# Modulation weights in eight column groups, and five projection units accumulated k by k at the start of a hybrid decoder block

## The reference

```
mod = c @ w_ada + b_ada                       # c: 1 x 1024, w_ada: 1024 x 3072
shift, scale, gate = split(mod, 3)
h = rmsnorm(x, pre_norm_gain) * (1 + scale) + shift        # 512 x 1024
proj = h @ w_in                                # split into aq ak av az iq ik iw bq bk bv bz bbeta ba ga gb
y_a = (dsa_attention(rope(aq), rope(ak), av, ...indexer of iq, ik, iw...) * silu(az)) @ w_a_out
y_b = (rmsnorm(gated_delta_rule(conv(bq), conv(bk), conv(bv), g, beta)) * silu(bz)) @ w_b_out
out = (sigmoid(ga) * y_a + sigmoid(gb) * y_b) @ w_o
return x + gate * rmsnorm(out, post_norm_gain)
```

## Time and profile before

| | us |
|---|---|
| median of 3 runs (827.45 to 828.1) | 827.98 |
| span of the profiled execution | 824.1 |
| PE busy | 797.4 |
| VectorE busy | 439.9 |
| GpSimd busy | 393.3 |
| ScalarE busy | 330.6 |

### The profile page before, as it was taken

One profiled execution on the slowest core, in us unless ns is written; L12 is line 12 of the kernel. 1 busy time (PEld: TensorE's weight loads), 2 busy tenths in 40 slices (PEclk: granted clock), 3 DMA queues, 4 the chain that ended last, 5 costly groups with the idle time before them and its releaser, 6 DMA issues.

```text
span 824.1 us, 11189 instructions
## 1 busy us (share of the span) xinstructions
PE 797.4 (97%) x4060; PEld 639.8 (78%) x4060; DVE 439.9 (53%) x957; ACT 330.6 (40%) x701; POOL 393.3 (48%) x338
## 2 busy tenths in 40 slices
PE   6899899999999999999999999999999999999997
PEld 2377775787887888888887777777778788878997
DVE  5677779848779855776754333343343332331113
ACT  0557455543544435445335334424443322122231
POOL 0415643465545644545554453554365355434451
PEclk9999999999999999999999999999999999999999
DMA  8936656543344333333212212222222255542602
GB/s 314 345 104 213 163 116 168 157 118 104 95 82 113 72 103 104 89 89 90 78 51 78 78 52 76 83 74 75 77 77 73 61 173 182 176 128 77 215 17 102
DMA packets 166800, 95.61 MB, mean 116 GB/s; under 512 B 35009, under 2 KB 158274, under 8 KB 165722
## 3 DMA queue, kind: packets, MB, share of 16 engines
q1 hardware_dynamic: 166746, 94.91, 40.2%
HBM read 85.11 MB, written 9.22 MB: 114 GB/s over the span
## 4 chain that ended last, share of the span: by engine, by line
PE 77%; DVE 11%; DMA 4%; ACT 4%; issue 2%; SPq 1%; POOL 1%; DVEq 0%; POOLq 0%; ACTq 0%
PE ps L699 19%; PE ps L701 18%; PE ps L700 18%; DMA w_ada_sb<-in_w_ada 2%; PE ps L979 2%; PE ps L1030 2%; PE ps L1029 2%; PE ps L1028 2%; PE ps L966 2%; ACT prob L1278 2%; DVE prob L1917 1%; PE ps L973 1%; PE ps L817 1%; DVE kraw L1734 1%; PE ps L863 1%
## 5 line engine op out<-in xcount | busy, mean ns | idle before, releaser
L1376 POOL TENSOR_TENSOR w_lo<-raw,w_hi 128x512 fp32r<-128x512 f32 (+1 forms) x216 | 294.7, 1388 | 305.0 <-ACT w_hi L1052 289.6
L699 PE MATMUL ps<-h_hi,w_hi 128*128 128x512 f32 (+1 forms) x680 | 286.2, 421 | 1.1 <-DVE h_lo L1597 1.0
L701 PE MATMUL ps<-h_hi,w_lo 128*128 128x512 f32 (+1 forms) x680 | 266.7, 392 | 0.0
L700 PE MATMUL ps<-h_lo,w_hi 128*128 128x512 f32 (+1 forms) x680 | 265.4, 390 | 0.0
L699 PEld LDWEIGHTS ps<-h_hi,w_hi 128*128 128x128 f32 (+1 forms) x680 | 127.8, 188 | 32.1 <-issue 8.3
L701 PEld LDWEIGHTS ps<-h_hi,w_lo 128*128 128x128 f32 (+1 forms) x680 | 127.3, 187 | 28.8
L700 PEld LDWEIGHTS ps<-h_lo,w_hi 128*128 128x128 f32 (+1 forms) x680 | 128.1, 188 | 23.0 <-issue 2.2
L1052 ACT ACTIVATE w_hi<-raw 128x1024 fp32r<-128x1024 f32 (+1 forms) x109 | 113.6, 1051 | 19.4 <-PE ps L1030 17.1
L1218 ACT ACTIVATE o_tok<-ps 128x128 f32<-128x128 f32 x32 | 8.9, 278 | 92.8 <-PE ps L931 92.7
L1029 PE MATMUL ps<-w_lo,y_hi 128*128 128x256 f32 x128 | 36.2, 283 | 0.0
L1030 PE MATMUL ps<-w_hi,y_lo 128*128 128x256 f32 x128 | 36.2, 283 | 0.0
(11 more groups left out here) (276 smaller groups left out, 1330.7 us busy)
## 6 DMA issues: line engine op xcount, KB each, us to landing
raw<-in_w_in SPq DMA_DIRECT2D x84, 512.0 KB, 3.7
w_ada_sb<-in_w_ada SPq DMA_DIRECT2D x8, 1024.0 KB, 11.4
inverse_tiles<-zero SPq DMA_DIRECT2D x12, 344.0 KB, 4.8
raw<-in_w_b_out SPq DMA_DIRECT2D x8, 512.0 KB, 3.8
raw<-in_w_a_out SPq DMA_DIRECT2D x8, 512.0 KB, 3.8
ada<-in_w_ada SPq DMA_DIRECT2D x8, 512.0 KB, 5.0
raw<-in_w_o SPq DMA_DIRECT2D x8, 512.0 KB, 3.8
x_sb<-in_x SPq DMA_DIRECT2D x4, 512.0 KB, 20.0
```

The lines of the kernel that those rows point to most:

```text
L699: pe.matmul(out_ap, w_hi[:, slot, k, 0:m], rhs_hi(k), start=(k == 0), stop=False)
L700: pe.matmul(out_ap, w_hi[:, slot, k, 0:m], rhs_lo(k), start=False, stop=False)
L701: mm = pe.matmul(out_ap, w_lo[:, slot, k, 0:m], rhs_hi(k), start=False, stop=(k == KT - 1))
L1376: ins = pool.tensor_tensor(w_lo[:, slot, ks, 0:n], raw[:, slot, ks, 0:n], w_hi[:, slot, ks, 0:n].bitcast(F32), ALU.subtract)
```

## The change

Inputs are now laid out on the host before the launch: the columns of `w_ada` for shift and scale in eight groups (`w_mod`, group k holds the 128 shift and 128 scale columns that eighth k of `h` needs, for all 1024 rows), the weights of the first five units by k (`w_first`), those of the others unit by unit (`w_units`), and all per-channel vectors in one tile (`first_cols`).

The opening becomes a loop over the eighths. For eighth k, 1 MB of `w_mod` and 0.33 MB of `w_first` arrive. The sum over the 1024 rows is made in two stages: ACT multiplies the first of eight row blocks by its part of `c`, DVE adds the seven others (`mod_sum`, seven instructions of 128 x 256), and two matmuls of one column by ones (`modulation`) add over the partitions and leave shift and scale as columns in PSUM. DVE adds the bias and gain (`mod_columns`, two instructions of 128 x 1). ACT then makes h and `h_hi`, POOL makes `h_lo`, ACT and POOL split the 128 x 640 weights of the five first units for this k, and PE does 15 matmuls (`first_units`): five with the rounded parts, then ten with the rests. `S` and `K0` to `K3` lie in five banks of their own. The matmuls of `w_ada` on PE and those without a reader are gone. The rotary tables are computed for the 24 distinct frequencies, widened by DVE, and transposed by 16 PE transposes, which ACT copies out.

From then on the rounds are as before, but round 0 starts after five units instead of two, so there are 12 rounds fewer. `R_KEY` lets K0 to K3 begin in rounds 1, 4, 7 and 10, units GA3 and GA4 come ahead of the first delta head, and DVE does `small` (the columns of S) ahead of the K taps of a round.

```diff
 RING = 4
-K_VEC = 5
+N_FIRST = 5
+GROUPS = 5
+FIRST_RAW = 3
...
-UNITS = ([("S", 0), ("K", 0)] + [("K", h) for h in range(1, 4)] + [("I", n) for n in range(4)]
...
+UNITS = ([("S", 0)] + [("K", h) for h in range(4)] + [("I", n) for n in range(4)]
+         + MIDDLE)
...
-R_KEY = [ends_at("K", h) for h in range(HEADS)]
-R_LOW = [10, 11, 12, 13, 30, 33, 46, 50]
-R_GRAM = [11, 12, 13, 16, R_DELTA[0] + 1, R_DELTA[0] + 6, R_DELTA[1] + 3, R_DELTA[1] + 7]
-R_INV = [24, R_DELTA[1] + 12]
+R_KEY = [1, 4, 7, 10] + [ends_at("K", h) for h in range(4, HEADS)]
+R_LOW = [8, 9, 10, 11, 22, 25, 38, 42]
+R_GRAM = [9, 10, 12, 16, R_DELTA[0] + 1, R_DELTA[0] + 6, R_DELTA[1] + 3, R_DELTA[1] + 7]
+R_INV = [20, R_DELTA[1] + 12]
...
+    def bank_of(q):
+
+        if PROJ_BANKS <= q < N_FIRST:
+            return q
+        return ((q - N_FIRST if q >= N_FIRST else q) + FIRST_BANK) % PROJ_BANKS
+
+    def before_in_bank(q):
+
+        return q - PROJ_BANKS if q >= N_FIRST + PROJ_BANKS else q - N_FIRST
...
+        sp.dma_start(pos_i[:], positions).then_inc(s_pos, 16)
...
+        def conditioning(k):
+            if k >= GROUPS:
+                sp.wait_ge(*pro_pe.at(f"mod{k - GROUPS}"))
+            for n in range(2):
+                half = slice(n * KT // 2, (n + 1) * KT // 2)
+                sp.dma_start(mod_rows[:, k % GROUPS, half, :], w_mod[k, :, half, :]).then_inc(s_mod[k % GROUPS][n], 16)
+
+        def first_weights(k):
+            if k >= FIRST_RAW:
+                sp.wait_ge(*pro_pool.at(f"wl{k - FIRST_RAW}"))
+            sp.dma_start(first_raw[:, k % FIRST_RAW], w_first[k]).then_inc(s_first[k % FIRST_RAW], 16)
+
+        for k in range(KT):
+            conditioning(k)
+            first_weights(k)
...
+        def first_units(k):
+
+            last = k == KT - 1
+            pe.wait_ge(*pro_act.at(f"wh{k}"))
+            pe.wait_ge(*pro_act.at(f"hi{k}"))
+            for q in range(N_FIRST):
+                pe.matmul(bank(bank_of(q)), first_hi[:, k, q, :], h_hi[:, k, :], start=(k == 0), stop=False)
+            if not last:
+                modulation(k + 1)
+            pe.wait_ge(*pro_pool.at(f"wl{k}"))
+            pe.wait_ge(*pro_pool.at(f"lo{k}"))
+            for q in range(N_FIRST):
+                pe.matmul(bank(bank_of(q)), first_lo[:, k, q, :], h_hi[:, k, :], start=False, stop=False)
+                mm = pe.matmul(bank(bank_of(q)), first_hi[:, k, q, :], h_lo[:, k, :], start=False, stop=last)
+                if last:
+                    mm.then_inc(unit_done, 1)
+                if q == 1 and k + 2 < KT:
+                    turn(k + 2)
...
+        def modulation(k):
+
+            if k == 0:
+                pe.wait_ge(*pro_pool.at("ones"))
+            else:
+                pe.wait_ge(*pro_dve.at(f"scale{k - 1}"))
+            pe.wait_ge(*pro_dve.at(f"row{KT - 1}_{k}"))
+            for n in range(2):
+                mm = pe.matmul(ps[:, 5, 2 * k + n:2 * k + n + 1], mod_rows[:, k % GROUPS, 0, n * P:(n + 1) * P], ones_p[:, 0:1],
+                               start=True, stop=True)
+            mm.then_inc(*pro_pe.inc(f"mod{k}"))
...
-        def condition(ks):
-            for k in ks:
-                pe.wait_ge(s_ada[k], 16)
-                for n in range(4):
-                    pe.matmul(bank(2 + n), cb[:, k, :], w_ada_sb[:, k, n * S:(n + 1) * S], start=(k == 0), stop=False)
-
-        pe.wait_ge(*pro_dve.at("cb"))
-        condition(range(2))
-        pe.wait_ge(s_rows2, 16 * 5)
-        pe.transpose(ps[:, 7, P:P + 3], prow2[:], ident[0:3, 0:3]).then_inc(*pro_pe.inc("rows2T"))
-        condition(range(2, K_VEC))
-        pe.wait_ge(*pro_pool.at("ones"))
-        pe.wait_ge(*pro_dve.at(f"acc{KT - 1}"))
-        for n in range(4):
-            mm = pe.matmul(bank(2 + n), ones_p[:], w_ada_sb[:, K_VEC, n * S:(n + 1) * S], start=False, stop=True)
-        mm.then_inc(*pro_pe.inc("mod"))
-        for _ in range(3):
-            pe.matmul(bank(0), cb[:, KT - 1, :], w_ada_sb[:, KT - 1, 0:S], start=True, stop=True)
...
+        def first_row(k):
+            act.wait_ge(s_mod[k % GROUPS][0], (k // GROUPS + 1) * 16)
+            act.activation(mod_rows[:, k % GROUPS, 0, :], mod_rows[:, k % GROUPS, 0, :], ACT.Copy,
+                           scale=pcol[:, 0, R_C:R_C + 1]).then_inc(*pro_act.inc(f"row{k}"))
+
+        act.wait_ge(s_rows, 16)
+        first_row(0)
+        act.wait_ge(*pro_pe.at("tables"))
+        act.wait_ge(s_cols, 16)
+        for t, (rows, name) in enumerate(((2 * N_AFREQ, "sinA"), (P, "sinI"))):
...
+            act.wait_ge(*pro_pe.at(f"x{k}"))
+            act.wait_ge(*pro_dve.at(f"scale{k}"))
+            if k >= 2:
+                act.wait_ge(*pro_pool.at(f"lo{k - 2}"))
+            act.activation(h_f32[:, k % 2, :], ps[:, 6 + k % 2, :], ACT.Identity, bias=small_cols[:, 8 + k:9 + k],
+                           scale=small_cols[:, 24 + k:25 + k]).then_inc(*pro_act.inc(f"h{k}"))
+            act.wait_ge(*pro_act.at(f"h{k}"))
+            act.activation(h_hi[:, k, :], h_f32[:, k % 2, :], ACT.Copy).then_inc(*pro_act.inc(f"hi{k}"))
+            if k + 2 < KT:
+                first_row(k + 2)
+                first_split(k + 2)
+            if k >= 6:
+                split(N_FIRST + k - 6)
 
...
+        def first_split(k):
+            pool.wait_ge(*pro_act.at(f"wh{k}"))
+            pool.tensor_tensor(first_lo[:, k], first_raw[:, k % FIRST_RAW], first_hi[:, k].bitcast(F32), ALU.subtract).then_inc(
+                *pro_pool.inc(f"wl{k}"))
+
+        first_split(0)
+        first_split(1)
+        for k in range(KT):
+            pool.wait_ge(*pro_act.at(f"hi{k}"))
+            pool.tensor_tensor(h_lo[:, k, :], h_f32[:, k % 2, :], h_hi[:, k, :].bitcast(F32), ALU.subtract).then_inc(
+                *pro_pool.inc(f"lo{k}"))
+            if k + 2 < KT:
+                first_split(k + 2)
+            if k >= 6:
+                split(N_FIRST + k - 6)
+        pool.wait_ge(*pro_pe.at(f"mod{KT - 1}"))
         pool.memset(zero[:], 0.0).then_inc(*pro_pool.inc("zero"))
...
-            dve.wait_ge(*pro_act.at(f"hi{k}"))
-            dve.tensor_tensor(h_lo[:, k, :], xT[:, k, :], h_hi[:, k, :].bitcast(F32), ALU.subtract).then_inc(
-                *pro_dve.inc(f"lo{k}"))
-            if k < 4:
-                extract(4 + k)
...
+        def mod_sum(k, js):
+
+            acc = mod_rows[:, k % GROUPS, 0, :]
+            for j in js:
+                if j == KT // 2:
+                    dve.wait_ge(s_mod[k % GROUPS][1], (k // GROUPS + 1) * 16)
+                if j == 1:
+                    dve.wait_ge(*pro_act.at(f"row{k}"))
+                else:
+                    dve.wait_ge(*pro_dve.at(f"row{j - 1}_{k}"))
+                dve.scalar_tensor_tensor(out=acc, in0=mod_rows[:, k % GROUPS, j, :], scalar=pcol[:, 0, R_C + j:R_C + j + 1], in1=acc,
+                                         op0=ALU.mult, op1=ALU.add).then_inc(*pro_dve.inc(f"row{j}_{k}"))
+
+        def mod_columns(k):
+
+            dve.wait_ge(*pro_pe.at(f"mod{k}"))
+            dve.tensor_tensor(small_cols[:, 8 + k:9 + k], ps[:, 5, 2 * k:2 * k + 1], pcol[:, 0, R_BADA + k:R_BADA + k + 1],
+                              ALU.add).then_inc(*pro_dve.inc(f"shift{k}"))
+            dve.scalar_tensor_tensor(out=small_cols[:, 24 + k:25 + k], in0=ps[:, 5, 2 * k + 1:2 * k + 2],
+                                     scalar=small_cols[:, 16 + k:17 + k], in1=pcol[:, 0, R_GAIN + k:R_GAIN + k + 1], op0=ALU.add,
+                                     op1=ALU.mult).then_inc(*pro_dve.inc(f"scale{k}"))
+
+        for i in range(3):
+            scale_rows(i)
+        mod_sum(0, range(1, 4))
         scale_rows(3)
+        mod_sum(0, range(4, KT))
         for k in range(KT):
-            if k == 4:
-                scales(1)
-            if k % 2 == 0:
-                dve.wait_ge(*pro_pe.at(f"x{k}"))
-                dve.tensor_scalar(xT[:, k, :], ps[:, [6, 7, 2, 4][k % 4], :], small_cols[:, 24 + k:25 + k],
-                                  small_cols[:, 8 + k:9 + k], ALU.mult, ALU.add).then_inc(*pro_dve.inc(f"h{k}"))
-            dve.wait_ge(*pro_act.at(f"hi{k}"))
-            dve.tensor_tensor(h_lo[:, k, :], xT[:, k, :], h_hi[:, k, :].bitcast(F32), ALU.subtract).then_inc(
-                *pro_dve.inc(f"lo{k}"))
-            if k < 4:
-                extract(4 + k)
-
-        dve.wait_ge(hi_made, 3)
-        dve.wait_ge(lo_made, 2)
-        dve.tensor_tensor(w_lo[:, 2], raw[:, 2], w_hi[:, 2].bitcast(F32), ALU.subtract).then_inc(lo_made, 1)
+            if k + 1 < KT:
+                mod_sum(k + 1, (1, 2))
+            mod_columns(k)
+            if k + 1 < KT:
+                mod_sum(k + 1, range(3, KT))
...
             for h in range(HEADS):
                 attend(h, r - R_ATT[h])
+            small(r)
             for h in range(HEADS):
                 rows(h, r - R_DELTA[h])
                 key(h, r - R_KEY[h])
                 attention_rows(h, r)
-            small(r)
             index_rows(r)
```

490 lines of the change are left out of this document (228 added, 262 removed).

## The result

The changed kernel takes 833.94 us (median of 5 runs, 832.09 to 836.31), the kernel before 827.98. The ratio is 1.0075, with a 95% interval of 1.0056 to 1.0093: slower, where 822.2 us and a gain had been forecast. The profiled execution has a span of 833.3 us.

A forecast was written before the change was run, and what follows sets the result against it. PE was taken as the bound, with room only in the opening. Round 0 at 65.0 plus 753.3 us behind it gave 818.3 us of span, plus 3.9 made 822.2 us; 8-in-10 range 810 to 828.5.

The forecast's parts named there:

- The opening: Start to round 0: VectorE with GpSimd sets the pace, about 5.8 us per eighth, round 0 at 65.0 us.
- the sign that the prediction had named: Opening row sums: about 0.4 us in most rows, 1.5 to 2 in one or two of seven.
- The exclusion of VectorE and GpSimd: Opening: VectorE instructions with two SBUF inputs and GpSimd's never run together; one eighth then costs 5.8 us.
- rival 1: Opening: the two engines overlap, PE sets passes of 4.1 us, round 0 near 54.7, total 811.9 us; chance 0.22.
- rival 3: Opening: PE's clock falls back, each slow eighth costs 2.5 us more, 832 us with four slow; chance 0.08.
- the term of 1.5 us for the rounds behind round 0: After round 0: added waits from the same side work in 48 rounds instead of 52, 1.5 us.
- Rival 2: After round 0: K0 and K1 bank waits not absorbed, VectorE behind for 48 rounds, +6 us, 828; chance 0.12.
- The offset: Whole kernel: the median time lies 3.9 us above the profiled span, added to 818.3 us.
- Three units fewer: After round 0: 72 matmuls at 0.227 us drop out, 16.3 us less, leaving 751.8 us if waits stay.

The follow-up runs named there:

- run 3: Changed kernel with both subtractions of each opening eighth (`h_lo`, `first_lo`) moved from GpSimd to VectorE: 830.81 us, ratio 1.0027.
- run 8: Changed kernel with ScalarE's inverse copy and the second inverse's first corner step two rounds later, plus the opening of run 3: 827.76 us, ratio 0.9993.
- Run 11: Kernel before the change with only the index logits four rounds earlier (from round 34 instead of 38): 833.98 us, ratio 1.0076.
- run 16: Run 14 with the second inverse's first corner step two rounds later, opening subtractions on VectorE and GpSimd's first split held back: 822.57 us, ratio 0.9929.
- run 1: Changed kernel with the index logits two rounds later (from round 34 instead of 32): 833.27 us, ratio 1.0045.
- run 5: Changed kernel with ScalarE's copy of the first finished inverse, and the store behind it, two rounds later: 832.85 us, ratio 1.0071.
- run 15: Changed kernel with ScalarE's inverse copy, the index logits and the second inverse's first corner step all two rounds later: 829.08 us, ratio 1.0007.
- run 13: Changed kernel with the first inverse's 30 row instructions working on one element each, leaving out part of the computation: 827.02 us, ratio 0.9988.
- run 14: Run 9 with the index logits two rounds later, from round 38 as before the change: 829.07 us, ratio 1.0008.
- run 6: Changed kernel with the first step of the second inverse's corner products two rounds later on VectorE: 829.53 us, ratio 1.0032.
- run 9: Changed kernel with a sixth gating unit before the first delta head, and logits, first inverse and later heads' decays four rounds later: 832.26 us, ratio 1.0067.
- run 10: Run 9 with the second inverse's first corner step two rounds later, opening subtractions on VectorE and GpSimd's first split held back: 827.39 us, ratio 0.9997.
- run 2: Changed kernel with one more gating unit (GA5) before the first delta head, side tasks left in their rounds: 835.73 us, ratio 1.0079.
- run 12: Kernel before the change with only the ring's unit weights laid out on the host, 4096 bytes per partition: 827.06 us, ratio 0.9992.

## Why the prediction was wrong

**The opening was right in its mechanism.** The seven row sums of an eighth took 5.75 us (L1606, one group of x7), in passes of 5.86 where 5.75 to 5.8 had been worked out, scale 0 came at 21.21 (21.3), scale 7 at 60.85 (59.8), round 0 at 66.81 (65.0). The 1.8 us are mostly the last pass (4.5 instead of 4.0) and the way from scale 7 to round 0 (6.0 instead of 5.2). In each of the passes of 5.86 five sums took 0.48 us and the two beside GpSimd's instructions 1.40 and 1.77, which is the sign that the prediction had named. The exclusion of VectorE and GpSimd is as read from the earlier trace rows, and run 3 confirms it from the other side: without GpSimd the sums take 0.49 each. That the passes came out so close is in part luck. Seven sums alone take 3.5 us and not 3.0, against which GpSimd adds 2.25 us and not the 2.4 of the sum, and the column steps hardly show (0.1, not 0.4). The slow clock of the opening (0.50 for 10.2 us from 18.6, matmuls 0.43 apart) cost nothing in the changed kernel, whose passes are 5.83 to 5.87 us in it and behind it. With the quicker passes of runs 3 and 8 it did cost: VectorE waited 1.3 and 2.1 us for PE's column sum. So rival 1 is out, and so is rival 3 as it was put: in the changed kernel the clock cost its time behind the opening, not in it.

The Trainium skill (SBUF — State Buffer, section Who interferes with whom) has the two engines shut each other out for whole instructions; by that rule the trace agrees, with 5.75 us for seven sums beside GpSimd and 3.5 without. It also tells of kernels in which a wait ahead of every short burst puts the clock back each time (TensorE: Matmul & The Clock Gate, section HAM oscillation). That did not come about here: the trace has one stretch of 10.2 us at 0.50 in the opening and full clock from 28.9 us on, though PE waits twice in every pass, some 0.5 us each time.

**The step that failed is the term of 1.5 us for the rounds behind round 0** ("With 48 rounds instead of 52 for the same side work until the first delta head, I add 1.5 us", with bounds of -2.5 and +6). It measured 14.7. Three things are in it.

- The place. The prediction looked at the rounds 0 to 16, where K0 to K3 are taken, and these were right (4.2 us of waits, 3.8 before). The four missing rounds lie behind them, and the logits moved by two more. `R_TURN + 8` is round 38, `R_DELTA[0] - 16` is round 32 (these two lines of the change are not among those shown above):

  ```
  -R_LOGIT = [R_TURN + 8 + 14 * (m // 2) // 11 for m in range(24)]
  +R_LOGIT = [R_DELTA[0] - 16 + 14 * (m // 2) // 11 for m in range(24)]
  ```

  That is six rounds less for an inverse of 11.3 us and two key convolutions. The prediction has no row of that stretch. Run 11 shows what was to be found in it: VectorE had not even four rounds to give there.
- The size. A few waits were taken as the price. The price is the stall (4.4 us), and on top the stretch at half clock (3.0 us). The same came again for the second stall (3.5 and 3.0). The clock was weighed for the opening alone.
- The second stall was in no rival. A wait of VectorE for a DMA, which lay unseen under PE's work (1.94 us before), grew by 2.2 us, two instructions behind it were stretched by 1.8 us more, and one step of VectorE that TensorE needs stood behind them.

Rival 2 came nearest, by one of its signs ("the distance from round 0 to the end is over 757", it is 766.5). Its mechanism was only half right: VectorE does fall behind, but not through the banks of K0 and K1 (1.1 us of waits for K taps), and not over all 48 rounds. Its +6 us were less than half of what it took, and the range ended at 828.5.

**The offset.** The median was taken 3.9 us over the profiled span. After, it is 833.94 - 833.3 = 0.6: the profiled execution of before was one of its quicker ones, that of after one of its slower ones (835.1 us, against a median of 833.94). That alone takes 3.3 us off, and hides a part of the miss: 1.8 (opening) + 13.2 (behind it) - 3.3 = 11.7 = 833.9 - 822.2.

**The idea of the change holds.** Three units fewer (16.3 us) with round 0 only 10.8 us later should give 5.5 us, and with the repaired opening of run 16, where round 0 is 4.7 us later, 11.6. Run 16 has 4.6 of them in its profile (819.5 against 824.1). What is missing is 758.7 instead of 751.8 us behind round 0, 5.7 of it idle time. Four stalls of 1.1 us are the largest part, at 338, 452, 482 and 484 us, where the kernel before had none. The changed kernel has two such, at 382.5 and 492.1. VectorE and GpSimd at the second:

```profile
489.75 2.32 DVE L1940 TENSOR_SCALAR prob<-prob,amx 128x128 f32<-128x128 f32 x4
```

```profile
490.53 2.68 POOL L1416 TENSOR_TENSOR w_lo<-raw,w_hi 128x512 fp32r<-128x512 f32 x2 [7.46 <-ACT w_hi L1070]
```

Four instructions take 2.32 us: three of them 0.29 to 0.41 each, and the last, at 490.55, 1.53, beside the GpSimd split that began just ahead of it. Where these two engines meet depends on how the side work lies against the units, and the change moved that. Whether it explains the other stalls was not tried.

## What to carry to other kernels

When work moves from a unit's place to the opening, count the rounds that every side task has left until its consumer, not only those next to the seam, and ask the trace of before how late the side engine is at the consumer. A stall behind an engine that has too much work is not mended by moving one waiting instruction: in the runs 1, 5 and 15 the next one came up, and only thinner work (13) or more rounds for all of it (14) helped. Moving one instruction did help where the engine stood waiting for a transfer (6). Price a stall of several microseconds with the slow stretch of TensorE behind it.

## What the runs showed of the hardware

- TensorE's granted clock falls in the middle of a kernel. In the changed kernel it stood at 0.50 for 6.8 us behind stalls of 4.36 and 3.48 us, at 3 us of lost work each. In the other runs it was 3.4 or 6.8 us behind stalls of 2.4 to 5.2 us, and the length did not follow the stall: 4.45 us brought 3.4 in run 6, and 2.38 brought 6.8 in run 15. Two stalls of 1.1 us near 490 us brought 3.4 or 6.8 us in the runs 9, 10 and 14, and nothing in the runs 2 and 16. The kernel before kept the full clock behind a stall of 2.55 us. In the runs 11 and 12 that same wait was 2.67 and 2.62 us, and 3.4 us at half clock followed.
- In run 8 the clock column reads 1.00 from 22 to 30 us, though the matmuls stood 0.43 apart, and it is the same in the openings of the runs 1, 2, 6, 9 and 15. As in the prediction, the spacing tells more than that column. Behind round 0, on which the account rests, no trace has a row of matmuls so spaced without the column at 0.50.
- VectorE with two SBUF inputs of 128 x 256 took 0.49 us alone and up to 1.77 beside GpSimd. With one input in SBUF (L1940, 128 x 512) it took 1.53 us beside GpSimd, where 128 x 384 took 0.41 just ahead. Taking work away from GpSimd and giving it to the engine that was the bottleneck made the opening 4.4 us shorter.
